# Two-block network on one core: modulation turned by VectorE, attention in rounds of two head halves, read-out's slab split earlier

## What is computed

```python
def ada_terms(cond, w_mod, b_mod):                      # w_mod: 1024 x 6144 for each of two layers
    m = jax.nn.silu(cond) @ w_mod + b_mod
    return jnp.split(m, 6, axis=-1)
...
sh1, sc1, gt1, sh2, sc2, gt2 = ada_terms(c[:, None, :], w_mod[layer], b_mod[layer])
a = modulate(rms_norm(h, g_mix_pre[layer]), sh1, sc1)    # ac: the same for the context, with c_ctx
y, yc = hybrid_mixer(a, ac, ...)
...
# hybrid_mixer: one projection a @ w_in gives two kinds of heads
#  A: 4 heads of 128, gated delta rule in both directions (short convolution, l2 norm, block inverse)
#  B: 8 query heads of 64 and 2 key/value heads of 64, over context and latent tokens (512 keys):
def attend(q, k, v):
    s = jnp.einsum("bqkgd,bskd->bkgqs", q, k) * (B_HEAD_DIM ** -0.5)
    p = jax.nn.softmax(s, axis=-1)
    return jnp.einsum("bkgqs,bskd->bqkgd", p, v)
y_lat = jnp.concatenate([delta_readout(o_lat_a, za_l, n_tok), o_lat_b], axis=-1) @ w_out
h = h + gt1 * rms_norm(y, g_mix_post[layer])
```

## Time and profile before

| | |
|---|---|
| timed runs, median | 2517.09 us |
| profiled execution, its own time | 2523.29 us |
| its span | 2521.5 us |
| PE busy | 2330.7 us (92%) |
| weight loads (PEld) | 2121.9 us (84%) |
| VectorE busy | 1597.1 us (63%) |
| ScalarE busy | 1116.2 us (44%) |
| GpSimd busy | 127.5 us (5%) |
| granted TensorE clock, mean | 0.959 |
| read from HBM | 364.62 MB, 145 GB/s over the span |

### The profile page before, as it was taken

The page is one execution under the profiler, slowest core; times in us unless marked ns, Lnnn a source line. Parts: engine busy times, 40 slices in busy tenths (PEclk is TensorE's granted clock), DMA queues, the critical chain, the costliest instruction groups (busy, mean ns, idle before and its releaser), DMA issues.

```text
span 2521.5 us, 41119 instructions
## 1 busy us (share of the span) xinstructions
PE 2330.7 (92%) x17410; PEld 2121.9 (84%) x17410; DVE 1597.1 (63%) x2601; ACT 1116.2 (44%) x1751; POOL 127.5 (5%) x130
## 2 busy tenths in 40 slices
PE   6998997999978999998998988998998998988997
PEld 3665686999867998988998978997668998987997
DVE  3376455554876655687556686655987656687555
ACT  3424335334345344744435445334555334745333
POOL 0011100000000000000000000002740000000000
PEclk9998998999989999998999989999999999998999
DMA  7245533554223554413554414553014554512551
GB/s 312 85 164 215 222 116 120 187 183 165 84 78 139 184 184 152 180 54 134 187 191 139 153 51 151 184 185 116 1 68 151 184 186 149 185 66 97 188 184 68
DMA packets 50296, 368.33 MB, mean 146 GB/s; under 512 B 5568, under 2 KB 5696, under 8 KB 5824
## 3 DMA queue, kind: packets, MB, share of 16 engines
q1 hardware_dynamic: 49968, 363.59, 39.9%
q10 hardware_dynamic: 144, 2.10, 0.2%
HBM read 364.62 MB, written 1.05 MB: 145 GB/s over the span
## 4 chain that ended last, share of the span: by engine, by line
PE 78%; DVE 14%; ACT 4%; issue 2%; DMA 1%; SPq 0%; DVEq 0%; ACTq 0%
PE psum L225 64%; DVE weight_parts L219 2%; PE psum L3680 1%; DMA weight_ring<-stream_dram 1%; PE psum L3681 1%; PE psum L2524 1%; DVE work L989 1%; PE psum L3009 1%; PE psum L407 1%; ACT weight_parts L193 1%; PE psum L552 1%; DVE work L984 1%; PE psum L1629 1%; DVE work L2833 1%; PE psum L3698 1%
## 5 line engine op out<-in xcount | busy, mean ns | idle before, releaser
L225 PE MATMUL psum<-input_parts,weight_parts 128*128 128x256 f32 x8448 | 1031.7, 285 | 47.6 <-DVE input_parts L997 27.0
L225 PEld LDWEIGHTS psum<-input_parts,weight_parts 128*128 128x128 f32 x8448 | 1024.8, 193 | 56.6 <-issue 50.8
L219 DVE TENSOR_TENSOR weight_parts<-weight_ring,weight_parts 128x1024 fp32r<-128x1024 f32 x536 | 631.9, 1220 | 274.6 <-ACT weight_parts L193 273.6
L193 ACT ACTIVATE weight_parts<-weight_ring 128x1024 fp32r<-128x1024 f32 x540 | 541.3, 1051 | 265.9 <-PE psum L225 265.1
L225 PE MATMUL psum<-hidden_parts,weight_parts 128*128 128x256 f32 x3936 | 481.1, 283 | 11.1 <-DVE hidden_parts L2650 6.6
L225 PEld LDWEIGHTS psum<-hidden_parts,weight_parts 128*128 128x128 f32 x3936 | 473.6, 190 | 16.3 <-issue 8.8
L1071 ACT ACTIVATE work<-psum 128x256 f32<-128x256 f32 x132 | 50.6, 383 | 422.1 <-PE psum L225 422.1
L1078 DVE TENSOR_TENSOR work<-work,psum 128x256 f32<-128x256 f32 x132 | 55.6, 421 | 282.3 <-ACT work L1071 282.3
L225 PE MATMUL psum<-work,weight_ring 128*128 128x256 f32 (+1 forms) x608 | 175.7, 448 | 3.5 <-ACT work L544 2.2
L225 PEld LDWEIGHTS psum<-work,weight_ring 128*128 128x128 f32 x608 | 118.3, 196 | 56.6 <-issue 43.1
L225 PE MATMUL psum<-weight_ring,silu_cond 128*32 128x256 f32 x768 | 56.5, 416 | 18.3 <-DMA weight_ring<-stream_dram 18.3
(11 more groups left out here) (465 smaller groups left out, 2369.4 us busy)
## 6 DMA issues: line engine op xcount, KB each, us to landing
weight_ring<-stream_dram SPq DMA_DIRECT2D x341, 1024.0 KB, 4.8
constants<-constants_dram SPq DMA_DIRECT2D x1, 2176.0 KB, 14.0
work<-s_bc_dram ACTq DMA_DIRECT2D x1, 2048.0 KB, 8.1
work<-ctx_dram SPq DMA_DIRECT2D x1, 1024.0 KB, 7.8
residual<-x_dram SPq DMA_DIRECT2D x1, 1024.0 KB, 9.8
out_dram<-residual SPq DMA_DIRECT2D x1, 1024.0 KB, 3.9
vectors<-vectors_dram SPq DMA_DIRECT2D x1, 550.5 KB, 3.7
constants<-constants_dram SPq DMA_DIRECT2D x1, 65.0 KB, 3.5
```

What stands on the lines that cost most here:

```text
L193: act.activation(self.parts[:, s % SPLITS, 0, cols], self.ring[:, i % RING, cols], ACT.Identity)\
L219: ins = dve.tensor_tensor(self.parts[:, s % SPLITS, 1, cols], self.ring[:, i % RING, cols], self.parts[:, s % SPLITS, 0, cols].bitcast(F32 ...
L225: mm = pe.matmul(*args, **kw)
```

## The change

Four things are changed together.

1. **Modulation.** A slab no longer holds 256 columns of w_mod for all 1024 rows, but 1024 columns (a "part", eight chunks of 128) for 256 rows; four slabs make a part (`by_parts`). `part_rows` multiplies one conditioning chunk with four groups of 256 columns, one to each strip, and accumulates over the eight chunks in `mod_bank`. So each strip holds finished sums for its own columns. `take_part` lets VectorE transpose the bank (32 x 32 blocks) and add the bias. ScalarE's copies, PE's turns and `strip_sum` are gone. PE's first matmul of a part waits until VectorE has transposed the part before.
2. **Where the background slabs lie.** 16 in the projection (two after each of chunks 5, 7, ... 19), 16 in attention, 8 in delta.
3. **Attention in rounds.** A round is a (j, t) with both halves: two score matmuls one after another on rows 0 to 63 and 64 to 127, a slab, the eight transposes of the round before, a slab. The value product is made once for each j, eight matmuls of 64 output columns, the halves on columns 0 to 63 and 64 to 127. Four probability buffers in place of two; the turned probabilities have one buffer for each half. `beside` is called twice behind each round.
4. **Read-out.** ScalarE rounds the attention half and the output projection's first slab before the delta output is squared, VectorE splits them before the norm.

```diff
-FILL_AFTER = range(5, 18, 2)
+FILL_AFTER = range(5, 20, 2)
+BESIDE_PROJECTION = 2 * len(FILL_AFTER)
...
+def part_rows(k, pe, i, slab, half, c):
+
+    if c == 0 and i:
+        pe.wait_ge(*k.part_taken[i - 1])
+    for j in range(STRIPS):
+        at = STRIP * j
+        mm = k.weights.matmul(pe, k.mod_bank[at:at + STRIP, 0:STRIP * KC], k.silu_c[:, c, :],
+                              slab[:, half, j * STRIP * KC:(j + 1) * STRIP * KC], start=(c == 0), stop=(c == KC - 1),
+                              tile_position=(0, at))
     return mm
...
+def take_part(k, dve, i, full, biased):
+
+    layer, part = divmod(i, COND // KC)
+    dve.wait_ge(*full)
+    dve.transpose(k.turned_part[:, :], k.mod_bank[:, 0:STRIP * KC]).then_inc(k.part_taken[i][0], 1)
+    dve.wait_ge(*k.part_taken[i])
+    rows = k.turned_part[:, :].rearrange("p (b r) -> p b r", r=STRIP)[:, :, 0:2]
+    bias = k.v("b_mod", layer * COND + part * KC, KC).unsqueeze(2).broadcast_to([P, KC, 2])
+    dve.tensor_tensor(k.mods[layer][:, part * KC:(part + 1) * KC, :], rows, bias, ALU.add).then_inc(biased[0], 1)
+    dve.wait_ge(*biased)
...
@@ Front.vector
+        dve.wait_ge(*self.loaded["vectors"])
+        take_part(k, dve, 0, self.full[0], self.biased[0])
         for i in range(2):
             dve.wait_ge(*self.x_loaded[i])
...
+        take_part(k, dve, 1, self.full[1], self.biased[1])
...
@@ HybridProjection.tensor
             if n in self.fill_after:
-                k.background.fill(pe, 2)
+                k.background.fill(pe, 4)
...
@@ HybridProjection.vector
         for i in range(4, 8):
             self.normalize(dve, i)
+        k.background.take(dve, STRIPS)
...
         self.lower.vector(dve, 2)
+        k.background.take(dve, 2 * STRIPS)
...
-        for i in range(8, 12):
+        for i in range(8, 10):
+            self.convolve(dve, i)
+        k.background.take(dve, 3 * STRIPS)
+        for i in range(10, 12):
             self.convolve(dve, i)
         self.blocks.early(dve)
+        k.background.take(dve, BESIDE_PROJECTION)
...
@@ HybridAttention.tensor
+        for r in range(len(self.rounds) + 1):
+            if r < len(self.rounds):
+                j, t = self.rounds[r]
+                jobs = self.score_jobs[2 * r:2 * r + 2]
+                for job in jobs:
+                    begin(pe, job)
+                for half, job in enumerate(jobs):
+                    rows = slice(64 * half, 64 * half + 64)
+                    pe.matmul(job.ap[:, :], self.q[rows, j, t * P:(t + 1) * P], self.kb[rows, :],
+                              start=True, stop=True).then_inc(job.full[0], 1)
+                k.background.fill(pe, 2)
+            if r >= 1:
+                for w in (2 * r - 2, 2 * r - 1):
+                    begin(pe, self.turn_jobs[w])
+                    pe.wait_ge(*self.probs_ready[w])
+                    for s in range(4):
+                        mm = pe.transpose(self.turn_jobs[w].ap[:, s * P:(s + 1) * P],
+                                          self.probs[:, w % 4, s * P:(s + 1) * P], k.c("ident"))
+                    mm.then_inc(self.turn_jobs[w].full[0], 1)
+            if r < len(self.rounds):
+                k.background.fill(pe, 2)
+            for i in self.heads_in(r):
+                k.hyb.sum_head(pe, i)
+            if r >= 2 and r % 2 == 0:
+                self.values(pe, r // 2 - 1)
+
+    def values(self, pe, j):
+
+        k, job = self.k, self.pv_jobs[j]
+        begin(pe, job)
+        if j == 0:
+            pe.wait_ge(*self.vt_ready)
+        pe.wait_ge(*self.pt_ready[4 * j + 3])
+        for s in range(4):
+            for half in range(2):
                 rows = slice(64 * half, 64 * half + 64)
...
+                mm = pe.matmul(job.ap[rows, 0:T], self.vt[:, s, rows], self.pt[:, half, s, :],
+                               start=(s == 0), stop=(s == 3), tile_position=(0, 64 * half))
+        mm.then_inc(job.full[0], 1)
...
@@ HybridAttention.scalar: both exponents of round r, then both copies of round r - 1
@@ HybridAttention.vector
+                for u in (2 * r, 2 * r + 1):
+                    dve.wait_ge(*self.score_jobs[u].full)
+                    k.dve.link(dve.reduce_max(k.cols[:, 3, u:u + 1], self.score_jobs[u].ap[:, :], AXX))
+                    dve.tensor_scalar(k.cols[:, 1, u:u + 1], k.cols[:, 3, u:u + 1], -0.125, None, ALU.mult)\
+                       .then_inc(self.peak[u][0], 1)
+                for u in (2 * r, 2 * r + 1):
+                    dve.wait_ge(*self.exp_done[u])
+                    k.dve.link(dve.reciprocal(k.cols[:, 3, u:u + 1], k.cols[:, 2, u:u + 1]))
+                    dve.tensor_scalar(self.probs[:, u % 4, :], self.probs[:, u % 4, :], k.cols[:, 3, u:u + 1],
+                                      None, ALU.mult).then_inc(self.probs_ready[u][0], 1)
+                k.background.take(dve, BESIDE_PROJECTION + 2 * r + 2)
+                self.blocks.beside(dve, 2 * r)
+                self.blocks.beside(dve, 2 * r + 1)
...
@@ DeltaReadout.scalar
+        act.wait_ge(*self.attention.out_ready[-1])
+        act.wait_ge(*self.delta.kv_jobs[5].full)
+        k.weights.round_through(act, self.next_slab)
+        act.wait_ge(*self.delta.ws_jobs[-1].full)
+        act.activation(self.parts[0][:, A_HEADS:KC, :], self.mix[:, A_HEADS:KC, :], ACT.Identity)\
+           .then_inc(self.hi_ready[0][0], 1)
         for i, t in enumerate(self.order):
             act.wait_ge(*self.delta.o_ready[i])
...
@@ DeltaReadout.vector: split_through(next_slab) stands in front of the norm instead of behind it
```

299 lines of the change are left out of this document (100 added, 199 removed).

## The result

The changed kernel ran in 2482.76 us, the median of four runs (2479.73 to 2488.08), beside 2517.83 us (2516.62 to 2525.45) for the kernel before on the same chip: a ratio of 0.9853, 95% interval 0.9832 to 0.9874: 1.5% faster. A later comparison gave 2482.02 us (five runs) against 2521.52 us, 0.9836 (0.981 to 0.9862). The forecast was 2480, faster, with 2464 to 2494 for its own case and 2464 to 2502 with the tiles' case; the time lies inside both. What is worth learning lies in the terms, two of which look wrong until both kernels are profiled twice, and in what the stage that gained most is bound by now.

The account below looks back on a forecast made before the run. PE was taken to bound projection, attention and delta, with the softmax chain binding attention's steady part afterwards. Terms -2.4 + 5.0 + 0.3 - 32 - 3.5 - 4.5 = -37 gave 2486 profiled, 2480 median; range 2464 to 2494.

Parts of the forecast that it names:

- Front: Stretch up to the projection's first matmul: turning matmuls and ScalarE copies go, VectorE transposes; -2.4 us (bounds -2.6 to -1.5).
- Projection: Projection stage: 16 slabs without turns replace 7 with 6 turns, +5.0 us on PE, plus 0.3 for the fourth taking.
- the rival at 2569: All stages with slabs: a slab's four strips lose their overlap, 3.4 us instead of 1.0, kernel slower at 2569; chance 0.04.
- Attention: Attention stage: rounds with both halves overlapping, ending near 267.5 and lasting 67 us; -32 us (bounds -38 to -25).
- the two additions: Attention: VectorE scalings slowed while GpSimd works, 3 us (0 to 5), and one fall of PE's clock, about 3 us.
- the rival at 2510: VectorE's takings of finished slab parts hold PE in every part, ten of 3 us each, giving 2510; chance 0.04.
- The pair of 11.2 us: Steady part of attention: a pair of heads takes 11.2 us through the softmax chain, against 21.3 before.
- The rival of tiles that don't overlap: Attention: scores cost 0.85 us more in 8 rounds, value products 1.7 in 4; +13.6 us, 2494; chance 0.10.
- The rival of a clock that stays low: Attention: low clock from round 1 to the end doubles PE's pieces of the chain; +22 us, 2502; chance 0.10.
- signs of being wrong: Observations that would count against the forecast: a slab above 1.1 us, score pairs of 1.9, or clock 0.50 past 245.
- Delta: Delta stage: eight turns of 0.4 to 0.5 us leave PE; -3.5 us, or -2 if VectorE's updates get in the way.
- Read-out: Read-out into output projection: slab and attention half prepared before the norm, PE starts earlier; -4.5 us (bounds -6 to -1).

Follow-up runs that it names:

- short_copies: Changed kernel with GpSimd's copies into the block matrices moving only an eighth of their elements; attention took 62.9 us.
- product_late: Changed kernel with each head pair's value product moved behind the next round's scores and first slab; attention took 59.8 us.
- after_again: Second profile of the changed kernel, nothing edited; projection 163.6 us, attention 65.3 us.
- attention_old: Changed kernel with attention's rounds undone, head halves one by one as before; 2510.26 us, 0.9963 of the kernel before, attention 94.4 us.
- one_half_tiles: Changed kernel with both halves of a head pair on the same rows and columns of TensorE; attention took 71.0 us.
- readout_old: Changed kernel with the read-out's slab rounded and split behind the norm again; norm's sums to output projection's first matmul 8.1 us, to next norm 40.3.
- before_again: Second profile of the kernel before the change, nothing edited; projection 160.5 us, attention 100.3 us, output projection 31.8 us.

## Why the prediction was right, point by point

**Front.** Forecast -2.4, first matmul near 34.8. It came at 34.32 and 35.31 in the two profiles, before at 37.16 and 37.35. VectorE's transpose, which no row of before had, took 0.45 where 0.4 was taken, and the bias followed it at 33.13 instead of 35.95:

```profile
32.65 0.45 DVE L407 STREAM_TRANSPOSE modulation_turned<-psum 128x256 f32<-128x256 f32 x1
33.13 0.17 DVE L411 TENSOR_TENSOR modulation<-modulation_turned,vectors 128x16 f32<-128x16 f32 x1
```

Plain scaling of rows 4 would have given 0.31; the 0.4 that was taken, a little above that end of the bounds, was nearer.

**Projection.** Forecast +5.3, scores at 200.4; the first profile says +1.3 and 196.0, the second +3.2 and 198.9. Taken alone the first is a term mis-sized by 4. But it holds a profile of before with the clock's fall at the gates against one of after without. Both profiles of before have the clock at 0.62 and 0.60 over their first 4 us and a chunk of 6.6 us behind the gates' matmuls. The changed projections with the same at both places are short_copies (165.2) and product_late (165.4): +4.8 and +5.0, nearly all of it behind the gates (110.6 to 110.7 us against 106.0). Eight pairs of slabs at 0.93 a slab are what was summed:

```profile
79.70 1.93 PE L225 MATMUL psum<-weight_ring,silu_cond 128*32 128x256 f32 x32
81.56 2.64 PE L225 MATMUL psum<-work,weight_ring 128*128 128x256 f32 x11
```

PE's work was sized rightly; what the prediction left out is that its base had a fall of the clock in it that the next execution need not have. A window of before at the gates would have shown it (0.50 at 92 to 96 us). That a slab might lose its overlap (the rival at 2569) is refuted by the row of 1.93 us for two slabs.

**Attention.** Forecast 67 us and -32; it took 67.8 and 65.3, -32.5 and -35.0. Here the steps can be followed, because each round begins with VectorE's first maximum (the timeline of VectorE, one row per round; round 4, at 232.81, is left out):

```profile
197.24 0.69 DVE L1646 TENSOR_REDUCE columns<-psum 128x1 f32<-128x512 f32 x1 [2.32 <-PE psum L1580]
...
207.65 0.69 DVE L1646 TENSOR_REDUCE columns<-psum 128x1 f32<-128x512 f32 x1
...
216.91 0.68 DVE L1646 TENSOR_REDUCE columns<-psum 128x1 f32<-128x512 f32 x1
...
225.18 0.69 DVE L1646 TENSOR_REDUCE columns<-psum 128x1 f32<-128x512 f32 x1 [0.70 <-PE psum L1580]
...
242.07 0.69 DVE L1646 TENSOR_REDUCE columns<-psum 128x1 f32<-128x512 f32 x1 [1.58 <-PE psum L1580]
...
248.28 0.69 DVE L1646 TENSOR_REDUCE columns<-psum 128x1 f32<-128x512 f32 x1
...
255.81 0.69 DVE L1646 TENSOR_REDUCE columns<-psum 128x1 f32<-128x512 f32 x1 [0.62 <-PE psum L1580]
```

Counted from the first, rounds 1 to 5 were forecast at 9.0, 18.7, 26.3, 34.1 and 41.0 us; they began at 10.4, 19.7, 27.9, 35.6 and 44.8. The first rounds are VectorE's, as said: in the rows of rounds 1 and 2 it has no wait ahead of the maximum. Of the 3.8 us that had gathered by round 5, 1.4 were there at round 1. They are ScalarE's: the first exponent began 4.1 us behind the first scores (200.13 and 196.01), and VectorE waited 2.03 us for it. The kernel before had the same 4.1 (201.69 and 197.57), but the prediction moved the exponent 1.0 later and the scores 2.8, so that it had ScalarE free some 1.8 us too early. The rest came in round 4, from a scaling beside GpSimd and a value product at half clock, with its scores (the timeline of PE):

```profile
236.35 3.68 PE L1608 MATMUL psum<-work 128*64 128x256 f32 x16 [3.59 <-ACT work L1634]
...
239.96 2.08 PE L1580 MATMUL psum<-work 64*128 64x512 f32 x4
```

Both kinds had been put into the sum apart, at 3 us each, and round 7, forecast at 52.2 without them, began at 58.6 in this profile and at 56.0 in the second: 6.4 and 3.8 late, the 1.4 of the first round included, where the additions allow 6. By the runs that keep step with after_again the first is 2.4 us and one fall of the clock behind a value product 1.8. So the walk through the rounds and the two additions were right in kind, each addition somewhat large for one fall and one contention, and the first round 1.4 too short. The waits for the takings, costed at nothing, are two, of 0.44 and 2.05 us (the second at 248.18), and the longer is the same contention again: the taking stood behind two long scalings. That refutes the rival at 2510, which had ten waits of 3 us.

The pair of 11.2 us was never reached in this execution: rounds 1 to 3 took 17.5, 3 to 5 16.9, and 5 to 7, the only ones that were to be steady, 13.7 (242.07 to 255.81), with two long scalings in them; in the second profile 13.2. The gain held since the sum had walked the early rounds one by one and not multiplied 11.2 by four. attention_old's expectation did the latter and missed by 13 us.

The Trainium skill, page TensorEngine Tiling (Array Packing), section PSUM Bottleneck, says that tiling relieves TensorE and not what takes the results out of PSUM. Here both sides of that can be measured: the value products halve (3.64 to 1.95), while undoing the tiles costs the stage only 3 to 6 us of the 13.6 that PE saves. The trace bears the sentence out in part: VectorE is busy 48.7 of 67.8 us, nearly as long as PE, but only its maxima, value copies and takings read PSUM, and its scalings and block steps, which are as much a part of its queue, do not.

The rival of tiles that don't overlap is refuted by one_half_tiles, and its price of 13.6 us was too high for the same reason; it would have been some 3 to 6. The rival of a clock that stays low is refuted by the windows: it fell several times, each time for a few microseconds (0.54 at 210 to 215, 0.66 at 220 to 225, 0.51 at 235 to 240), and came back once PE was busy. Three of the prediction's signs of being wrong did show, at half clock alone, and cost little: score pairs of 1.93 and 2.08 us, slabs of 1.93, and a clock of 0.50 past 245 (the window of PE in the first profile; at 255 to 260 it is 1.00 again, and the second profile has 1.00 here):

```profile
250.00:252.00 2.00, 2.00 (x16) 0.50 0.93 332
```

DMA was costed at nothing: 250 GB/s over the stage, and no wait of PE for a slab in it.

**Delta.** Forecast -3.5; 83.2 became 79.3 in both profiles, -3.9. The eight turns of rows 13 are 0.4 to 0.5 each, which fits; no run undoes them alone.

**Read-out.** Forecast -4.5. The first pair of profiles says -6.5 up to the next norm, outside the bounds of -6 to -1. The part of it that the edit explains is the start, 8.0 to 3.5; readout_old gives 4.7 for the whole. The other 2.0 come from the output projection itself (34.2 against 32.1), and before_again has 31.8 there: the first profile of before had a longer fall of the clock behind its wait. Against before_again the term is -4.2 (39.8 to 35.6), and the forecast right. Windows of the same 4 us, the first profile of before and then the second:

```profile
392.00:396.00 4.00, 4.00 (x23) 4.00 (x23) 1.47 (x2) 0.00 (x0) 0.00 (x0) 0.60 1.03 412
```

```profile
392.00:396.00 4.00, 4.00 (x35) 4.00 (x35) 1.71 (x2) 0.00 (x0) 0.00 (x0) 0.99 1.02 430
```

**The sum.** The prediction's bounds of the terms, added, give -45 to -24, not -50 to -24; nothing hangs on it. Up to the next norm the two profiles of each kernel differ by 43.3 us on average (422.2 and 378.9), where 37 were forecast: the projection cost 3 less than forecast, attention gave 2 more, the read-out 1. Behind it the untouched program takes 2096.6 to 2098.3 us in the two profiles of before, and 2099.6 to 2103.1 in the twelve of kernels with the change or parts of it, some 3.7 us more. All twelve are longer, so it is hardly chance. Nearly half lies in one stretch of the second network: 187.4 us in both profiles of before (1937.48 to 2124.88 in the first), 189.2 in both of the changed kernel (1893.39 to 2082.57), the clock at 1.00 in all four, so the clock is not its cause. No run tells what is, and it stays open. The net is 40 by the profiles, and 35.1 and 39.5 by the medians. That the prediction met the median so closely owes something to this: a stage sum that was about 6 too small and a loss of 3 to 4 that was not foreseen.

## What to carry to other kernels

Work a stage whose bound changes hands round by round through its start; a steady period multiplied by the number of rounds misses what costs most, the rounds in which another engine has extra work. Row and column tiles of TensorE halve PE's pieces, but the stage then falls only to what its vector work allows: find next the step whose copy PE waits for and move PE's use of it a round later, which gave 5.5 to 8 us of the stage here. And before a term of a few microseconds is read from two profiles, look at the granted clock behind each pause in both, take a second profile of each kernel, and compare the runs that keep step with each other up to the place that was edited.

## What the runs showed of the hardware

A pause of PE of 2.05 us, in the same place of the same code, was followed by full clock in four executions and by 0.50 in six, and the chunk behind it took 3.72 us or 5.4 to 6.8. At the start of the same stage the clock over the first 4 us was 1.00 in two of these ten, 0.53 to 0.65 in six and 0.50 in two. The Trainium skill, page TensorE: Matmul & The Clock Gate, Part 1, ties the clock to how busy PE has been; these traces agree, and show besides that the same pause goes either way, so that a profile's stage can differ by 3 to 4 us with nothing changed.

Two matmuls of 64 rows and 512 columns on different rows of TensorE, in fp32, take 1.13 us together, and 1.98 on the same rows. Two groups of eight matmul instructions with 64 output columns each, 256 wide, take 1.95 together and 3.64 one after another on the same columns.

In the changed kernel a VectorE scaling of 128x512 from SBUF to SBUF takes 0.49 us alone, up to 1.98 beside GpSimd's copies and 1.47 to 1.73 beside its clearing of memory; five of sixteen were hit in each of its two profiles. The maxima out of PSUM in the same stretch took 0.64 to 0.69, as elsewhere.
